# Split operands for the scores and value products of the second block's attention, with scores two units ahead

## Chip, core and metric

The kernel runs on one core of a Trainium2 chip. The metric is the device time of one execution in microseconds, median of the runs. TensorE (PE) multiplies, VectorE (DVE) and ScalarE (ACT) work element by element, GpSimd (POOL) helps, SyncE (SP) issues the transfers.

## What is computed

A first transformer block runs over 256 tokens, then a second block of two layers over the same 256 tokens (x) and 256 context tokens. Everything is float32. The change touches the second block's attention, whose core is:

```python
def latent_attention(q, k, v, k_ctx, v_ctx):
    keys = jnp.concatenate([k_ctx, k], axis=1)
    vals = jnp.concatenate([v_ctx, v], axis=1)
    ...
    s = jnp.einsum('bqhgd,bkhd->bhgqk', q_blk, keys, ...) * scale
    p = jax.nn.softmax(s, axis=-1).astype(vals.dtype)
    return jnp.einsum('bhgqk,bkhd->bqhgd', p, vals)
```

It has 8 heads of 128 dimensions over 2 key-value heads. Queries and keys are normalised per head, those of x are also rotated by position. Layer 0 also attends from the context tokens to themselves.

## The kernel before

Each engine has its own hand-written program; semaphores (`S("name")`) join them. An engine runs its instructions in order, so one that waits holds up all behind it. Matmuls with weights use split operands: ScalarE rounds a float32 tile to a high part (type fp32r), VectorE subtracts it from the original for the low part, and `product` issues three matmuls, high by high, high by low, low by high. Scores, products with values and transposes use plain float32; the records show two matmuls for each such product and one for each transpose.

**Projection (`WIN`).** A layer runs 12 weight chunks (q = 0 to 11), each in two halves of 24 matmuls on PE. Work of other kinds sits between the halves (`within(q)`). Chunks 7 to 10 give the four pairs of query heads, chunk 11 the values and keys rest (`kv10`). After each query chunk ScalarE copies the pair, squares it (HSQ) and multiplies the gain in (`query_pair`). PE sums the squares over the 128 dimensions (`query_sums`, L2447): the squares are the loaded operand and one column of ones streams. VectorE and POOL rotate keys and pairs (`rotated(r)`, L1647 to L1652: shuffle, sine product, a wait for POOL's cosine product, sum). At q = 11 VectorE does `rotated(3)` and, in layer 0, `rotated(4)`, then the low part of a weight chunk (L1233), the reciprocal roots, `maxima(0)` and `gated_lo` (L1715).

**Units.** A unit is a head for 256 queries. Layer 0 has 16: units 0 to 7 with 512 keys, 8 to 15 (context) with 256; layer 1 has 8, with 512. For each unit: PE computes scores (`scores2`, L2508 or L2510); VectorE takes maxima (L1733, L1736); ScalarE takes exponentials with their sums (L1086); VectorE normalises (`normalise2`, L1742 and L1745, tile PB); PE transposes the probabilities (L2615); ScalarE copies them (L1133, tile PT2, two buffers); PE multiplies by the values (`values`, L2522); VectorE copies the result (`attended`, L1751). PE's turn in the loop is scores of u + 1, values of u - 1, transposes of u. In unit 0 PE also transposes the values (L2590) and ScalarE copies them (L1138). During the last two units and after, PE fills in products of the other branch (`hyena_tiles`). Then come the merge, output and feed-forward projections.

The output projection has four chunks (`out`); after the last, VectorE updates X (L1868) and a norm follows.

## Time and profile before

| what | us |
|---|---|
| median of 3 runs | 1856.95 |
| lowest to highest | 1856.34 to 1860.36 |
| the profiled execution, whole | 1852.7 |
| its span in the profile | 1850.9 |
| PE busy in it | 1808.2 (98%) |
| DVE busy | 1078.3 (58%) |
| ACT busy | 796.0 (43%) |
| layer 0's units (first to last transposes) | 762.4 to 823.0 |
| layer 1's units | 1508.0 to 1542.4 |

A busy share tells how long an engine had work in flight. The profiled execution took 4.25 us less than the median, so a sum made on the profile is moved by that much to stand beside the median. In a timeline, the difference between two starts on PE is what an instruction costs its queue; its own duration is longer, since matmuls overlap.

### The profile page before, as it was taken

How to read it: one execution, taken by the hardware profiler on the slowest of the kernel's cores; microseconds unless marked ns; L12 is line 12 of the kernel's file. 1: busy time of each engine (PE TensorE's matmuls, PEld its weight loads, DVE VectorE, ACT ScalarE, POOL GpSimd, SP SyncE). 2: the span in 40 equal slices, each digit the busy share in tenths (PEclk: the TensorE clock that was granted, in tenths of full speed). 3: DMA queues.
4: the chain of work that ended last, by engine and by line, in shares of the span. 5: the costliest groups of instructions: out<-in, count | busy, mean ns of one | idle time of the engine just before them, and what ended most of it. 6: DMA issues, size and time to landing. Idle time of an engine off the chain costs nothing.

```text
span 1850.9 us, 27019 instructions
## 1 busy us (share of the span) xinstructions
PE 1808.2 (98%) x11122; PEld 1552.6 (84%) x11122; DVE 1078.3 (58%) x1268; ACT 796.0 (43%) x1003; POOL 139.3 (8%) x122
## 2 busy tenths in 40 slices
PE   7999998999999999999999999999999999999998
PEld 6889895888998888777878788888888979988898
DVE  5776475677667565654334447754227775466564
ACT  6444435454446433554323422222226455355543
POOL 3000211300004110101000100000001010000000
PEclk9999999999999999999999999999999999999999
DMA  9875487777543321103224268773324423556651
GB/s 280 232 228 208 134 275 258 230 200 214 184 152 120 102 75 63 46 23 110 91 92 112 78 201 256 225 234 112 111 71 154 137 69 105 185 144 182 194 192 68
DMA packets 310626, 284.46 MB, mean 154 GB/s; under 512 B 9108, under 2 KB 290339, under 8 KB 307453
## 3 DMA queue, kind: packets, MB, share of 16 engines
q1 hardware_dynamic: 308394, 278.05, 48.0%
q0 software_dynamic: 1904, 4.89, 0.8%
q8 instruction: 77, 1.26, 0.3%
q14 instruction: 24, 0.20, 0.0%
q10 hardware_dynamic: 227, 0.06, 0.0%
HBM read 280.71 MB, written 2.12 MB: 153 GB/s over the span
## 4 chain that ended last, share of the span: by engine, by line
PE 88%; DVE 4%; ACT 3%; issue 1%; POOL 1%; DMA 1%; ACTq 0%; DVEq 0%; SPq 0%
PE PS L1933 20%; PE PS L1935 20%; PE PS L1934 20%; PE PS L1978 11%; PE PS L1979 6%; PE PS L2522 1%; PE PS L2508 1%; ACT PB L1086 1%; DVE WLO L1233 1%; ACT WHI L754 1%; DMA RAW<-in_ffn_w_gu_dram 1%; PE PS L2105 1%; POOL X L692 1%; PE PS L2615 1%; PE PS L2120 1%
## 5 line engine op out<-in xcount | busy, mean ns | idle before, releaser
L1233 DVE TENSOR_TENSOR WLO<-RAW,WHI 128x2048 fp32r<-128x2048 f32 x209 | 484.9, 2321 | 313.9 <-ACT WHI L754 313.5
L754 ACT ACTIVATE WHI<-RAW 128x2048 fp32r<-128x2048 f32 x209 | 398.9, 1910 | 261.5 <-PE PS L1935 241.5
L1933 PE MATMUL PS<-AHL,WHI 128*128 128x512 f32 (+1 forms) x1424 | 489.9, 344 | 4.2 <-DVE AHL L1363 2.0
L1935 PE MATMUL PS<-AHL,WLO 128*128 128x512 f32 (+1 forms) x1424 | 481.1, 338 | 0.0
L1934 PE MATMUL PS<-AHL,WHI 128*128 128x512 f32 (+1 forms) x1424 | 481.1, 338 | 0.0
L1978 PE MATMUL PS<-AHL,WHI 128*128 128x512 f32 x1056 | 373.6, 398 | 3.8 <-DVE AHL L1363 2.0
L1933 PEld LDWEIGHTS PS<-AHL,WHI 128*128 128x128 f32 x1424 | 269.9, 190 | 42.0 <-issue 9.2
L1979 PE MATMUL PS<-AHL,WLO 128*128 128x256 f32 x1056 | 296.9, 281 | 0.0
L1934 PEld LDWEIGHTS PS<-AHL,WHI 128*128 128x128 f32 x1424 | 270.1, 190 | 29.4 <-issue 1.2
L1935 PEld LDWEIGHTS PS<-AHL,WLO 128*128 128x128 f32 x1424 | 270.0, 190 | 29.2
L1978 PEld LDWEIGHTS PS<-AHL,WHI 128*128 128x128 f32 x1056 | 199.8, 189 | 53.4 <-issue 7.4
L1933 PE MATMUL PS<-SHI,WHI 128*128 128x256 f32 (+1 forms) x704 | 219.9, 312 | 0.8 <-DVE SLO L1239 0.8
L1934 PE MATMUL PS<-SLO,WHI 128*128 128x256 f32 (+1 forms) x704 | 218.0, 310 | 0.0
L1935 PE MATMUL PS<-SHI,WLO 128*128 128x256 f32 (+1 forms) x704 | 217.9, 310 | 0.0
L1979 PEld LDWEIGHTS PS<-AHL,WLO 128*128 128x128 f32 x1056 | 201.4, 191 | 0.1
L1933 PEld LDWEIGHTS PS<-SHI,WHI 128*128 128x128 f32 x704 | 134.3, 191 | 12.1 <-issue 5.0
L1935 PEld LDWEIGHTS PS<-SHI,WLO 128*128 128x128 f32 x704 | 134.3, 191 | 6.8
L1934 PEld LDWEIGHTS PS<-SLO,WHI 128*128 128x128 f32 x704 | 134.3, 191 | 6.7
L1203 ACT ACTIVATE SIL<-PS 128x512 f32<-128x512 f32 x22 | 13.2, 599 | 181.0 <-PE PS L1935 180.9
L1898 DVE TENSOR_TENSOR HB<-SIL,PS 128x512 f32<-128x512 f32 x22 | 15.1, 687 | 92.9 <-ACT SIL L1203 92.9
L836 ACT ACTIVATE GU<-PS 128x512 f32<-128x512 f32 x44 | 26.2, 595 | 98.8 <-PE PS L1979 96.7
L1286 DVE SCALAR_TENSOR_TENSOR LACC<-LRAW,SC,LACC 128x1024 f32<-128x1024 f32 x56 | 68.3, 1278 | 0.0
(305 smaller groups left out, 1885.8 us busy)
## 6 DMA issues: line engine op xcount, KB each, us to landing
RAW<-in_w_in_dram SPq DMA_DIRECT2D x98, 512.0 KB, 4.5
RAW<-in_ffn_w_gu_dram SPq DMA_DIRECT2D x88, 512.0 KB, 5.4
RAW<-in_w_gate_up_dram SPq DMA_DIRECT2D x88, 512.0 KB, 5.1
MRAW<-in_w_mod_dram SPq DMA_DIRECT2D x24, 1024.0 KB, 8.2
LRAW<-in_w_mod_dram SPq DMA_DIRECT2D x48, 512.0 KB, 4.8
RAW<-in_ffn_w_down_dram SPq DMA_DIRECT2D x44, 512.0 KB, 4.3
RAW<-in_w_down_dram SPq DMA_DIRECT2D x44, 512.0 KB, 4.2
RAW<-in_w_out_dram SPq DMA_DIRECT2D x24, 512.0 KB, 4.5
```

The lines of the kernel that those rows point to most:

```text
L692: pool.tensor_tensor(X[:, k, 0:TX], X[:, k, 0:TX], TU[:, k, :], ALU.add).then_inc(S("xu"), 1)
L754: act.activation(WHI[:, c % RING, :], RAW[:, c % RING, :], ACT.Copy).then_inc(S("hi_done"), 1)
L836: act.activation(GU[:, j % RING, :, :], ringw(j)[:, :, TX:TB], ACT.Copy).then_inc(S("gu_lo"), 1)
L1086: act.activation(PB[:, s, t, 0:n], src, ACT.Exp, scale=RC[:, col:col + 1], bias=NM[:, s, t:t + 1], accum_out=SMX[:, s, t:t + 1]).then_inc( ...
L1233: dve.tensor_tensor(WLO[:, c % RING, :], RAW[:, c % RING, :], WHI[:, c % RING, :].bitcast(F32), ALU.subtract)\
L1286: dve.scalar_tensor_tensor(out=LACC[a][:, :, :], in0=raw, scalar=col, in1=LACC[a][:, :, :], op0=ALU.mult, op1=ALU.add).then_inc(S("mod_acc ...
L1933: pe.matmul(out, whi, xhi, start=first, stop=False, skip_group_check=shared)
L1934: pe.matmul(out, whi, xlo, start=False, stop=False, skip_group_check=shared)
L1935: return pe.matmul(out, wlo, xhi, start=False, stop=last, skip_group_check=shared)
L1978: pe.matmul(out[:, b, :], whi, both[:, :, a, 0:TX], start=a == 0, stop=False, skip_group_check=True)
L1979: last = pe.matmul(out[:, b, 0:TX], wlo, both[:, 0, a, 0:TX], start=False, stop=a == KT - 1, skip_group_check=True)
L2105: last = pe.matmul(PS[32 * b:32 * b + 32, 7, :], SC[:, at:at + 32], MRAW[mod_slot(t)][:, b, :], start=t == 0, stop=t == MAIN - 1)
```

## The change

Scores and products with values use split operands. ScalarE makes high queries (QHI, a block b of two heads each), high keys (KHI), and writes PT2 and the transposed values VT2 as high parts; VectorE makes the low parts QKLO (in the place of the originals), PT2LO and VT2LO. PT2 now has one buffer. `attended` moves from VectorE to ScalarE. Scores run two units ahead. The query sums of the first three pairs now load a 32-column selector and stream the squares, each token tile into a group of 32 output partitions of its own; the roots are taken earlier for these (`early_roots`), turned by one transpose (`roots_turned`), and a second reciprocal is added. In layer 1's last output chunk the two output tiles get separate banks, and the first is updated halfway. Cut to its core:

```diff
...
-        VT2 = at("VT2", [P, 8, P], 128 * K)
+        QKLO = at("QKLO", [P, 12, TB], A, F32R)
+        QHI = at("QHI", [P, 4, 2, TX], A + 24 * K, F32R)
+        KHI = at("KHI", [P, 2, TB], 140 * K, F32R)
+        VT2, VT2LO = at("VT2", [P, 8, P], 128 * K, F32R), at("VT2LO", [P, 8, P], 192 * K, F32R)
...
-        PT2 = at("PT2", [P, 2, 4, TX], A + 40 * K)
+        PT2, PT2LO = at("PT2", [P, 4, TX], A + 40 * K, F32R), at("PT2LO", [P, 4, TX], A + 44 * K, F32R)
...
+                return [PS[:, 0, 0:TX], PS[:, 1, 0:TX]]
+            return [ring2(j, n)[:, t, :] for t in range(2)]
...
+                def early_roots():
+                    act.wait_ge(S("h_ss"), 6 * layer + 4)
+                    act.activation(QROOT[0:32 * tq, :], PS[0:32 * tq, 7, TX:TX + P], ACT.Sqrt, bias=EPSC[0:32 * tq, 1:2])\
+                       .then_inc(S("h_std"), 1)
...
+                def keys_hi():
+                    act.wait_ge(S("h_sum"), 5 * layer + 1)
+                    if layer == 0:
+                        act.wait_ge(S("y_fwd"), 4)
+                    act.activation(KHI[:, :, :], QKV[:, 8:10, :], ACT.Copy).then_inc(S("qk_hi"), 1)
+                def queries_hi(b):
+                    heads, tokens = query_block(b)
+                    if b < 4:
+                        act.wait_ge(S("h_sum"), 5 * layer + 2 + b)
+                    if b == 0:
+                        act.wait_ge(S("y_h"), y_done)
+                    elif b >= 4:
+                        act.wait_ge(S("b_s"), u0 + 2 * b - 6)
+                    act.activation(QHI[:, b % 4, :, :], QKV[:, heads, tokens], ACT.Copy).then_inc(S("qk_hi"), 1)
+                def attended(u):
+                    grp, h = units[u]
+                    act.wait_ge(S("b_pv"), u0 + u + 1)
+                    act.activation(QKV[:, h, TX * grp:TX * grp + TX], PS[:, 6 + u % 2, 0:TX], ACT.Copy).then_inc(S("b_o"), 1)
...
+                        early_roots()
+                        queries_hi(1)
...
                         exps(0)
+                        exps(1)
...
+                    if u % 2 == 0 and u and u // 2 + 2 < len(units) // 2:
+                        queries_hi(u // 2 + 2)
...
+                    if u:
+                        act.wait_ge(S("b_pv"), u0 + u)
...
-                        exps(1)
-
+                        queries_hi(2)
+                    else:
+                        attended(u - 1)
+                attended(len(units) - 1)
...
+                def keys_lo():
+                    dve.wait_ge(S("qk_hi"), split_count(layer, -1))
+                    dve.tensor_tensor(QKLO[:, 8:10, :], QKV[:, 8:10, :], KHI[:, :, :].bitcast(F32), ALU.subtract).then_inc(S("qk_lo"), 1)
...
+                    dve.wait_ge(S("qk_hi"), split_count(layer, b))
+                    dve.tensor_tensor(QKLO[:, heads, tokens], QKV[:, heads, tokens], QHI[:, b % 4, :, :].bitcast(F32), ALU.subtract)\
+                       .then_inc(S("qk_lo"), 1)
...
+                def turned_lo(u):
+                    kts = 4 if units[u][0] == 0 else 2
+                    dve.wait_ge(S("b_pt"), u0 + u + 1)
+                    dve.tensor_tensor(PT2LO[:, 0:kts, :], PS[:, 4:4 + kts // 2, :].rearrange("p a (b n) -> p (a b) n", n=TX),
+                                      PT2[:, 0:kts, :].bitcast(F32), ALU.subtract).then_inc(S("b_pl"), 1)
+                    if u == 0:
+                        dve.wait_ge(S("v_ev"), layer + 1)
+                        dve.tensor_tensor(VT2LO[:, :, :], PS[:, 6:8, :].rearrange("p a (b n) -> p (a b) n", n=P),
+                                          VT2[:, :, :].bitcast(F32), ALU.subtract).then_inc(S("b_pl"), 1)
...
                     normalise2(u)
-                    if u + 1 < len(units):
-                        maxima(u + 1)
-                    if u == 0 and layer == 1:
-                        rotated(4)
-                    if u:
-                        attended(u - 1)
+                    if layer == 1 and u < 2:
+                        summed(u + 3)
+                    if u + 2 < len(units):
+                        maxima(u + 2)
+                    if layer == 1 and u == 0:
+                        turned_round(4)
+                    if u % 2 == 0 and u // 2 + 2 < len(units) // 2:
+                        queries_lo(u // 2 + 2)
+                    turned_lo(u)
...
-                        if j == 3 and t == 0 and layer == 0:
-                            dve.wait_ge(S("out_half"), 1)
+                        if j == 3 and t == 0:
+                            dve.wait_ge(S("out_half"), layer + 1)
...
-                            last = pe.matmul(PS[:, 7, TX + h * tq + t:TX + h * tq + t + 1], HSQ[:, h % 2, t * P:t * P + P], ONES[:, 0:1],
-                                             start=True, stop=True)
+                            squares = HSQ[:, h % 2, t * P:t * P + P]
+                            if pair < 3:
+                                last = pe.matmul(PS[32 * t:32 * t + 32, 7, TX:TX + P], SEL[:, 7 - h:39 - h], squares,
+                                                 start=h == 0, stop=h == 5)
...
+                    pe.wait_ge(S("h_std"), 3 * layer + 2)
+                    pe.transpose(PS[:, 7, TX + P:TX + P + 32 * tq], QROOT[0:32 * tq, :], IDENT[0:32 * tq, 0:32 * tq])\
+                      .then_inc(S("h_ss"), 1)
...
+                    pe.wait_ge(S("qk_lo"), split_count(layer, u // 2))
                     for t in range(2):
-                        q = QKV[:, h, TX * grp + t * P:TX * grp + t * P + P]
-                        if grp == 0:
-                            last = pe.matmul(PS[:, 2 * (u % 2) + t, :], q, QKV[:, 8 + h // 4, :], start=True, stop=True)
-                        else:
-                            last = pe.matmul(PS[:, 2 * (u % 2), TX * t:TX * t + TX], q, QKV[:, 8 + h // 4, TX:TB], start=True, stop=True)
+                        q0 = TX * grp + t * P
+                        out = PS[:, 2 * (u % 2) + t, :] if grp == 0 else PS[:, 2 * (u % 2), TX * t:TX * t + TX]
+                        keys = slice(TX * grp, TB)
+                        last = product(out, QHI[:, u // 2 % 4, h % 2, t * P:t * P + P], QKLO[:, h, q0:q0 + P],
+                                       KHI[:, h // 4, keys], QKLO[:, 8 + h // 4, keys], True, True)
...
-                        pe.wait_ge(S("v_ev"), layer + 1)
+                        pe.wait_ge(S("b_pl"), u0 + layer + 2)
                     if u >= 2:
                         pe.wait_ge(S("b_o"), u0 + u - 1)
                     kts = range(4) if grp == 0 else range(2, 4)
+                    out = PS[:, 6 + u % 2, 0:TX]
                     for a, kt in enumerate(kts):
-                        last = pe.matmul(PS[:, 6 + u % 2, 0:TX], VT2[:, 2 * kt + h // 4, :], PT2[:, u % 2, a, :],
-                                         start=a == 0, stop=a == len(kts) - 1)
+                        pe.matmul(out, VT2[:, 2 * kt + h // 4, :], PT2[:, a, :], start=a == 0, stop=False)
+                    for a, kt in enumerate(kts):
+                        pe.matmul(out, VT2LO[:, 2 * kt + h // 4, :], PT2[:, a, :], start=False, stop=False)
+                    pe.wait_ge(S("b_pl"), u0 + layer + u + 2)
+                    for a, kt in enumerate(kts):
+                        last = pe.matmul(out, VT2[:, 2 * kt + h // 4, :], PT2LO[:, a, :], start=False, stop=a == len(kts) - 1)
...
+                    if q == 11:
+                        roots_turned()
                     if 8 <= q <= 11:
                         query_sums(q - 8)
                     if q == 11:
                         scores2(0)
+                        scores2(1)
...
-                scores2(1)
                 for u, (grp, h) in enumerate(units):
                     last_two = u - len(units) + 2
-                    if u and u + 1 < len(units):
-                        scores2(u + 1)
+                    if u + 2 < len(units):
+                        scores2(u + 2)
                     if u:
                         values(u - 1)
                     if u == 0:
                         pe.wait_ge(S("qkv_ev"), 6 * layer + 6)
                     pe.wait_ge(S("b_p"), 2 * (u0 + u) + 2)
+                    if u:
+                        pe.wait_ge(S("b_pl"), u0 + layer + u + 1)
...
```

VectorE at q = 11 of layer 0, before. QKV are queries and keys, BR the rotation's scratch tile, WLO a weight chunk's low part, RC reciprocal roots, NM maxima, HLO the other branch's low part:

```order
L1647 STREAM_SHUFFLE BR<-QKV 128x512
L1649 TENSOR_TENSOR BR<-BR,ROPE 128x512
L1652 TENSOR_TENSOR QKV<-QKV,BR 128x2x256
L1233 TENSOR_TENSOR WLO<-RAW,WHI 128x2048
L1723 RECIPROCAL RC<-STD 128x32
L1733 TENSOR_REDUCE NM<-PS 128x2
L1736 TENSOR_TENSOR NM<-NM,RC 128x2
L1715 TENSOR_TENSOR HLO<-HY,HHI 128x512 x4
L1742 RECIPROCAL RS<-SMX 128x2
```

These begin with the second of two rotations. And in the changed kernel, from the same rotation:

```order
L1708 STREAM_SHUFFLE BR<-QKV 128x512
L1710 TENSOR_TENSOR BR<-BR,ROPE 128x512
L1717 TENSOR_TENSOR QKV<-QKV,BR 128x2x256
L1810 TENSOR_TENSOR QKLO<-QKV,QHI 128x2x256
L1295 TENSOR_TENSOR WLO<-RAW,WHI 128x2048
L1793 RECIPROCAL RC<-PS 128x24
L1796 RECIPROCAL RC<-STD 128x8
L1818 TENSOR_REDUCE NM<-PS 128x2
L1821 TENSOR_TENSOR NM<-NM,RC 128x2
L1818 TENSOR_REDUCE NM<-PS 128x2
L1821 TENSOR_TENSOR NM<-NM,RC 128x2
L1785 TENSOR_TENSOR HLO<-HY,HHI 128x512 x4
```

A low part of queries, a reciprocal and a second maxima came in; another `QKLO<-QKV,QHI` stands ahead of the first of the two rotations.

VectorE in unit 0 of layer 0, changed (before: RS, PB, NM, NM only):

```order
L1827 RECIPROCAL RS<-SMX 128x2
L1830 TENSOR_SCALAR PB<-PB,RS 128x512 x2
L1818 TENSOR_REDUCE NM<-PS 128x2
L1821 TENSOR_TENSOR NM<-NM,RC 128x2
L1810 TENSOR_TENSOR QKLO<-QKV,QHI 128x2x256
L1837 TENSOR_TENSOR PT2LO<-PS,PT_123 128x1024
L1841 TENSOR_TENSOR VT2LO<-PS,VT_119 128x1024
```

Three subtractions now stand behind the maxima and ahead of the next unit's RS.

PE in one of layer 0's later units, changed (before: two scores, four products, eight transposes, in the same turn). KHI and QHI are high parts, QKLO low ones:

```order
L2033 MATMUL PS<-KHI,QHI 128x512
L2034 MATMUL PS<-QKLO,QHI 128x512
L2035 MATMUL PS<-KHI,QKLO 128x512
...
L2631 MATMUL PS<-PT_123,VT_119 128x256 x4
L2633 MATMUL PS<-PT_123,VT2LO 128x256 x4
L2636 MATMUL PS<-PT2LO,VT_119 128x256 x4
L2732 MATMUL PS<-IDENT,PB 128x128 x8
```

The last four products read PT2LO, which VectorE makes after ScalarE's copy; the next transposes stand behind them.

## Rows read from the trace of the kernel before

**Rows 1.** The page, part 4: the chain that ended last, by engine.

```profile
...
PE 88%; DVE 4%; ACT 3%; issue 1%; POOL 1%; DMA 1%; ACTq 0%; DVEq 0%; SPq 0%
...
```

**Rows 2.** Timeline of PE, layer 0's units: start us, us, group xcount, [idle before <-releaser].

```profile
...
762.40 1.04 PE L2615 MATMUL PS<-IDENT,PB 128*128 128x128 f32 x8
...
768.16 1.09 PE L2615 MATMUL PS<-IDENT,PB 128*128 128x128 f32 x8 [0.41 <-DVE PB L1745]
...
773.89 1.04 PE L2615 MATMUL PS<-IDENT,PB 128*128 128x128 f32 x8
...
779.09 1.88 PE L2508 MATMUL PS<-QKV 128*128 128x512 f32 x4
780.80 1.93 PE L2522 MATMUL PS<-PT,VT 128*128 128x256 f32 x8
782.57 1.04 PE L2615 MATMUL PS<-IDENT,PB 128*128 128x128 f32 x8
...
795.56 1.04 PE L2615 MATMUL PS<-IDENT,PB 128*128 128x128 f32 x8
...
```

**Rows 3.** Timeline of PE, layer 0's units of 256 keys.

```profile
...
801.79 0.60 PE L2615 MATMUL PS<-IDENT,PB 128*128 128x128 f32 x4
...
816.18 0.60 PE L2615 MATMUL PS<-IDENT,PB 128*128 128x128 f32 x4
...
```

**Rows 4.** Timeline of PE, layer 1: transposes of the first two units.

```profile
...
1508.02 1.06 PE L2615 MATMUL PS<-IDENT,PB 128*128 128x128 f32 x8 [1.32 <-DVE PB L1745]
...
1513.81 1.09 PE L2615 MATMUL PS<-IDENT,PB 128*128 128x128 f32 x8 [0.41 <-DVE PB L1745]
...
```

**Rows 5.** The chain in order of time, 700 to 860 us: query sums, start us, us.

```profile
...
739.12 1.68 PE PS L2447 x16
...
```

**Rows 6.** The chain in order of time, 1450 to 1660 us: key sums and query sums.

```profile
...
1462.49 0.57 PE PS L2427 x16
...
1481.01 0.79 PE PS L2447 x8
...
```

**Rows 7.** Timeline of PE, rounded operands, 512 columns.

```profile
...
757.05 0.40 PE L1935 MATMUL PS<-AHL,WLO 128*128 128x512 f32 x1
757.28 0.39 PE L1933 MATMUL PS<-AHL,WHI 128*128 128x512 f32 x1
...
```

**Rows 8.** Timeline of PE, rounded operands, 256 columns.

```profile
...
1461.98 0.28 PE L1933 MATMUL PS<-AHL,WHI 128*128 128x256 f32 x1
1462.10 0.28 PE L1934 MATMUL PS<-AHL,WHI 128*128 128x256 f32 x1
...
```

**Rows 9.** Groups by line, 700 to 860 us, DVE and ACT: busy us, mean ns | idle.

```profile
...
L1836 DVE TENSOR_TENSOR MG<-MG,SG 128x1024 f32<-128x1024 f32 x1 | 1.2, 1225 | 5.9 <-ACT SG L1164 5.9
...
L1133 ACT ACTIVATE PT<-PS 128x1024 f32<-128x1024 f32 x8 | 8.1, 1018 | 2.4 <-PE PS L2615 2.4
...
L1133 ACT ACTIVATE PT<-PS 128x512 f32<-128x512 f32 x8 | 4.7, 593 | 4.3 <-PE PS L2615 4.3
...
L1067 ACT ACTIVATE HHI<-HY 128x512 fp32r<-128x512 f32 x4 | 2.2, 616 | 0.0
...
```

**Rows 10.** Timeline of DVE, layer 0, last projection chunk and first units.

```profile
...
749.71 0.01 DVE L1647 LOAD_MASK_SELECT BR<-QKV  x1 [2.40 <-ACT QKV L1034]
...
752.42 0.69 DVE L1652 TENSOR_TENSOR QKV<-QKV,BR 128x512 f32<-128x512 f32 x1 [1.25 <-POOL QKV L729]
...
759.36 0.15 DVE L1742 RECIPROCAL RS<-SMX 128x2 f32<-128x2 f32 x1
...
780.00 0.88 DVE L1745 TENSOR_SCALAR PB<-PB,RS 128x512 f32<-128x512 f32 x2
781.00 1.22 DVE L1733 TENSOR_REDUCE NM<-PS 128x2 f32<-128x1024 f32 x1
...
```

**Rows 11.** Timeline of DVE, layer 1, last output chunk.

```profile
...
1646.71 0.88 DVE L1868 SCALAR_TENSOR_TENSOR X<-PS,MOD,X 128x256 f32<-128x256 f32 x2 [2.23 <-PE PS L1935]
...
```

**Rows 12.** Window in layer 1: busy us of PE, PEld, DVE, ACT, POOL; granted clock.

```profile
...
1650.00:1655.00 5.00, 3.16 (x14) 2.66 (x14) 4.36 (x12) 2.83 (x6) 0.00 (x0) 0.57 0.03 8
...
```

More of the change, by code:

```diff
@@ L397, in ring2, with split_count, query_block, out_tiles @@
             return PS[:, s:s + 2, :] if n == TB else PS[:, s, :].rearrange("p (t n) -> p t n", t=2)
+        def split_count(layer, b):
+            return 9 * layer + 2 + b
+        def query_block(b):
+            return slice(2 * (b % 4), 2 * (b % 4) + 2), slice(TX * (b // 4), TX * (b // 4) + TX)
+        def out_tiles(j, n):
+            if n == TX and j == 3:
+                return [PS[:, 0, 0:TX], PS[:, 1, 0:TX]]
+            return [ring2(j, n)[:, t, :] for t in range(2)]
         def win_out(layer, c):
@@ L1029, in query_pair @@
                         act.wait_ge(S("h_kn"), 2)
-                    act.wait_ge(S("h_ss"), 5 * layer + pair + 1)
+                    act.wait_ge(S("h_ss"), 6 * layer + pair + 1)
                     act.wait_ge(S("qkv_ev"), 6 * layer + pair + 2)
@@ L1091, in _ @@
                     c = FIRST[f"win{layer}"] + q
+                    if q == 11:
+                        queries_hi(0)
                     split_w(None, c + AHEAD)
+                    if q == 9 and layer == 0 or q == 10 and layer == 1:
+                        keys_hi()
                     if layer == 0 and q == 0:
@@ L1653, in rotated @@
                        .then_inc(S("h_sum"), 1)
+                def rotated(r):
+                    turned_round(r)
+                    summed(r)
                 def tapped(q, m0):
@@ L1746, in normalise2 @@
                            .then_inc(S("b_p"), 1)
-                def attended(u):
-                    grp, h = units[u]
-                    dve.wait_ge(S("b_pv"), u0 + u + 1)
-                    dve.tensor_copy(QKV[:, h, TX * grp:TX * grp + TX], PS[:, 6 + u % 2, 0:TX]).then_inc(S("b_o"), 1)
+                def turned_lo(u):
[7 more added lines that the diff above has]
+                                          VT2[:, :, :].bitcast(F32), ALU.subtract).then_inc(S("b_pl"), 1)
                 for q, (kind, m0) in enumerate(WIN[layer]):
@@ L1793, in _ @@
                             rotated(2)
+                            keys_lo()
                     if q == 11:
-                        rotated(3)
+                        queries_lo(0)
                         if layer == 0:
+                            rotated(3)
                             rotated(4)
+                        else:
+                            turned_round(3)
+                        queries_lo(1)
                         split_w(None, FIRST[f"win{layer}"] + q + AHEAD)
@@ L1800, in _ @@
                         maxima(0)
+                        maxima(1)
                         gated_lo()
@@ L2093, in later_rows @@
                         for b in range(4):
-                            last = pe.matmul(PS[32 * b:32 * b + 32, 6, TX * half:TX * half + TX], SEL[:, 5 - x:37 - x], LACC[a][:, b, :],
+                            last = pe.matmul(PS[32 * b:32 * b + 32, 6, TX * half:TX * half + TX], SEL[:, 7 - x:39 - x], LACC[a][:, b, :],
                                              start=part == 0 and x == 0, stop=r == 2, skip_group_check=True)
@@ L2663, in _ @@
                         pe.wait_ge(S("xo"), 2 * KT * layer + 2 * (nt // TX))
-                    out = ring2(j, nt)
                     def first_tile(last):
-                        if layer == 0:
-                            last.then_inc(S("out_half"), 1)
+                        last.then_inc(S("out_half"), 1)
                         norm_sums(9 + 2 * layer, nt // P, SQ2, range(4))
-                    by_columns(None, FIRST[f"out{layer}"] + j, [out[:, 0, :], out[:, 1, :]], AHI2, ALO2, nt,
+                    by_columns(None, FIRST[f"out{layer}"] + j, out_tiles(j, nt), AHI2, ALO2, nt,
                                ready=wait_k("mg_lo", KT * layer) if j == 0 else None, between=first_tile if j == 3 else None)
```

56 lines of the change are left out of this document (32 added, 24 removed).

## Prediction

> **What bounds the kernel now.** I read the page's chain first: 88% of the end-setting chain is PE [rows 1]. So an edit counts by what it does to PE's queue, and elsewhere only where PE comes to wait. Then I read PE's timeline through the units of layer 0. In the steady state scores (start 779.09), products (780.80) and transposes (782.57) stand back to back: 1.71 + 1.77 + 0.87 us, a unit every 4.33 us, with no wait [rows 2]. The first units are slower: transposes start at 762.40, 768.16 and 773.89, steps of 5.76 and 5.73 us, since exponentials, copy and products follow one another there [rows 2]. From the third (773.89) to the eighth (795.56) are five steps, 21.67 us. The 256-key units go from 801.79 to 816.18 in five steps of 2.88 us [rows 3]. Layer 1 starts as layer 0: 1508.02 to 1513.81, 5.79 us [rows 4]. I call the transposes of unit u T(u).
>
> **Part 1, query sums.** A pair in layer 0 now holds PE for 1.68 us (16 records) [rows 5]. The nearest row to the new form is the key sums: also 32 loaded columns, 128 streamed, four output groups, 16 records, 0.57 us [rows 6]. Three pairs save 3 x 1.11 = 3.3 us. VectorE and ScalarE wait on PE in that stretch, so all moves forward. In layer 1 a pair costs 0.79 us [rows 6] and uses two output groups. Bounds per pair: nothing saved, or down to half of 0.57, 0.29. I take half of 0.79 and a little, 0.43: 0.36 each. Only pairs 0 and 1 help, since the wait behind pair 2 is VectorE's; about 0.75 us. The Trainium skill (TensorEngine Tiling (Array Packing), Theoretical Speedup) allows a factor of up to 4 for a dimension of at most 32. By it layer 0's pairs would cost 0.42 us and save 3.8; the row shows a factor of 2.9.
>
> **Part 2, matmuls.** Rounded matmuls start 0.23 us apart with 512 columns [rows 7], 0.12 us with 256 [rows 8]. Scores take 6 x 0.227 = 1.36 us for 1.71, products 12 x 0.12 = 1.44 for 1.77; leaving and entering plain float32 costs about 0.08 us each time: the last matmul starts at 1462.10 [rows 8], the key sums by 1462.49 [rows 6] and not 0.12 later. PE's work in a unit falls to 1.36 + 1.44 + 0.87 + 0.16 = 3.83 us. If PE stayed the bound, each step would gain 0.5 us. It does not, by part 3.
>
> **Part 3, the new loop.** PT2 has one buffer and PT2LO is made from the same PSUM banks that the next transposes write. So this circle closes once per unit: T(u), ScalarE's copy, VectorE's low part, VectorE's normalisation of unit u + 1 (queued behind it), T(u + 1). Transposes take 1.04 us [rows 2] and 0.09 to be seen; the copy 1.02 [rows 9] + 0.04; the low part reads PSUM and SBUF, 1024 elements: the subtraction's nearest row is 1.23 us [rows 9], 1.15 of it in the queue; normalisation 0.20 + 0.88 [rows 10] + 0.06. Sum 4.48 us a step, against 4.33. VectorE's maxima (1.22 us [rows 10], 1.33 with its small product) and a 512-element low part of queries (0.69 us, 0.62 in the queue [rows 10]) fit beside transposes and copy. ScalarE, 43% busy over the span, takes on `attended` and high queries; both lie beside VectorE's part of the circle. With 256 keys the circle is 0.60 + 0.09 [rows 3], 0.59 + 0.04 [rows 9], 0.61, 0.88: 2.81, against 2.88.
>
> **Part 4, the start in layer 0.** `queries_lo(0)` stands ahead of `rotated(3)` on VectorE and needs `queries_hi(0)`, which ScalarE reaches only after the last pair's gain, the release at 749.71 [rows 10]. Before, `rotated(3)` was done by then and only `rotated(4)` was left. So ahead of the first normalisation (759.36 [rows 10]) VectorE's chain gains: high queries 0.62 [rows 9], low queries twice 0.62, a rotation 749.71 to 752.42 + 0.61 = 3.3 [rows 10] and 0.2 of its own wait, a second reciprocal 0.2, a second maxima 1.33. Together 6.9 us: normalisation at 766.3, T(0) at 767.4, for 762.40 now; +5.0. PE stands idle for some of it, while scores of unit 2 go by.
>
> From T(0) to T(1): transposes 1.13, copy 0.92 and value copy 0.92 (queue), `queries_hi(2)` 0.66, and then on VectorE `queries_lo(2)` 0.62, low probabilities 1.15, low values 1.29, for both of which `values(0)` waits, then the products 1.52: 8.2 us for 5.76, +2.45. T(1) to T(2): 4.48 for 5.73, -1.25. To T(7): 5 x 4.48 = 22.4 for 21.67, +0.7. T(7) to T(9): one mixed step 4.2 and 2.81 for 6.23, +0.8. Then five of 2.81: -0.3. Behind it products filled in cover the waits, and the last two products give 0.1. Sum +7.3; with part 1, **+4.0 us in layer 0**.
>
> **Part 5, layer 1.** Only the first half of `rotated(3)` stays ahead, so VectorE's chain grows by low keys 1.15 + 2 x 0.62 + 0.2 + 1.33 = 3.9 and loses the wait for POOL and the sum, 1.25 + 0.61 [rows 10], and 0.2: +1.8. T(0) also needs the copy of kv10, now behind two units' exponentials on ScalarE; both chains end within 0.5 us of each other, and I take +1.7. Less 0.75 from part 1: +0.95. T(0) to T(1) 8.2 for 5.79, +2.4; to T(2) -1.25; four steps +0.6; the last, filled with products, and the end -0.3. **+2.4 us.** Halving the last output chunk's update takes one of two (0.88 us together [rows 11]) off the path: -0.4. The key copy and low keys in layer 0 lie under PE's halves of chunks 9 and 10; uncovered they would cost 2.2 us. The longer way to the first a2_lo adds 0.6 us on ScalarE, under 5.5 us of products.
>
> **Sum.** +4.0 + 2.4 - 0.4 = +6.0 us on the profiled execution's 1852.7. Beside the median, 4.25 us higher, that is **1863 us**, 0.3% slower.
>
> **Rival A, the clock falls.** In the output norm of layer 1, where PE had 3.16 of 5 us of work, the granted clock was 0.57, so that part ran at 1.2 GHz for 2.4 [rows 12]. My schedule leaves PE idle about 1.6, 1.7 and 3.5 us around T(0) and T(1). A clock of 0.57 over 5 us is 4.3 us at half speed; PE's 3.83 us of a unit then take 7.7 for 4.48, and 4.3 us at that rate lose 1.8; with a tail as long again up to 2.9 a layer. Both layers: 1863 + 3.6 to 5.8, about 1868. Against: PE stood idle 1.32 us ahead of layer 1's T(0), and its first step, 5.79 us, is no longer than layer 0's 5.76 [rows 2, 4]. The Trainium skill (TensorE: Matmul & The Clock Gate, The HAM clock gate) says that the array goes to 1.2 GHz when it has been idle; by that rule this is the outcome. Chance 0.2.
>
> **Rival B, the start costs no more than now.** The mechanism: scores two ahead let exponentials and maxima run during the wait, and VectorE, idle there before, takes its subtractions in gaps, so that T(0) to T(1) stays at 5.8 us. That is -2.4 in each layer, 1858: within the noise. The order speaks against it: the subtractions stand in series behind the copies. Chance 0.17.
>
> **Rival C, cheap subtractions (faster).** One mechanism: the low parts cost half of the row's 1.23 us. Then the circle is 3.9 us, T(0) to T(1) loses 1.5, the start 0.5 and 1.1. Layer 0: 6 x 0.55 + 1.5 + 0.5 + 6 x 0.27 = 6.9; layer 1: 5 x 0.55 + 1.5 + 1.1 = 5.3. Sum -12: 1851, faster. It decides from about 0.7 us for 1024 elements on. Against: 512 elements take 0.69 and 1024 take 1.23, proportionally. Chance 0.08.
>
> **Rival D, no gain from the sums** in spite of the key sums: +3.3 + 0.75, 1867. Chance 0.07.
>
> **How the numbers follow.** The forecast keeps 0.48, with its own range of 1860.5 to 1865.5 (some 0.1 us a step over 18 steps, 0.5 for the starts). What a measurement can tell from no change is 0.2%, 3.7 us: 1853.2 to 1860.7. Faster is rival C, 0.08. Same is rival B and a small share of the forecast, 0.24. Slower is the rest, 0.68. The range of 1857.5 to 1869 leaves out C and the far tail of A.
>
> **What would show it.** Right: T(u) steps of 4.4 to 4.6 us in layer 0 with VectorE busy or awaited in each; `QKLO<-QKV,QHI` waiting for ScalarE at the head of chunk 11; T(0) to T(1) near 8.2 us; the first three pairs' sums near 0.6 us. Wrong: steps under 4.2, which would mean that subtraction or copy is cheaper than its row; T(1) less than 7 us behind T(0); an idle gap in chunks 8 to 10 of either layer, which would say that the sums' gain was not handed on; or a granted clock under 0.9 in the units, rival A.

## The result and the profile after

| | us |
|---|---|
| before, median of 10 runs beside the change | 1856.1 |
| after, median of 10 runs | 1865.3 |
| after to before | 1.0048, 95% interval 1.0039 to 1.0057 |
| the profiled execution after, whole (its span) | 1865.7 (1863.9) |

The change costs 9.2 us; forecast were 1863.0 us and a range of 1857.5 to 1869. The two profiled executions lie 13.0 us apart, more than the medians, so I set landmarks. The first is PE's `UNFOLD` product of chunk 8 (706.41 us before, 708.43 after). All the matmuls ahead of it are the same in both, so the 2.0 us there belong to the execution, not to the change. "Net" below means with this shift taken off.

| stretch, us | before | after | forecast of the difference | measured |
|---|---|---|---|---|
| landmark to T(0), layer 0 | 55.99 | 57.69 | +1.7 | +1.70 |
| T(0) to T(1) | 5.76 | 9.45 | +2.45 | +3.69 |
| T(1) to T(2) | 5.73 | 4.46 | -1.25 | -1.27 |
| T(2) to T(7), five steps | 21.67 | 22.29 | +0.7 | +0.62 |
| T(7) to T(9) | 6.23 | 6.99 | +0.8 | +0.76 |
| T(9) to T(14), five steps | 14.39 | 13.97 | -0.3 | -0.42 |
| T(14) to T(15) | 6.78 | 8.31 | -0.1 | +1.53 |
| T(15) to layer 1's T(0) | 685.06 | 687.18 | +0.95 | +2.12 |
| layer 1's T(0) to T(7) | 34.33 | 37.32 | +1.5 | +2.99 |
| from there to the end | 308.55 | 307.81 | -0.4 | -0.74 |

Five of the terms hit within 0.12 us. Of those that were exceeded, three hold stretches of low clock (T(0) to T(1), T(14) to T(15), and layer 1's first steps), and the fourth is the start of layer 1. Without the 2.0 us ahead of the landmark and the 1.5 us at T(14), which did not come back in a second profile (e8), the two profiles lie 9.5 us apart, near the 9.2 of the medians.

The chain of work that ended last, in order of time (start, us, engine and tile), layer 0, after. It shows T(0) at 766.12, then all that stands ahead of the first products, and one steady step (784.49 to 788.95):

```profile
766.12 1.08 PE PS L2732 x8
767.24 0.04 issue
767.28 1.02 ACT PT L1192
768.30 0.92 ACT VT L1197
769.22 0.52 ACT QHI L1118
769.77 0.69 DVE QKLO L1810
770.46 1.14 DVE PT2LO L1837
771.59 1.14 DVE VT2LO L1841
772.73 0.14 issue
772.87 1.20 PE PS L2631 x4
...
784.49 1.11 PE PS L2732 x8
785.62 1.04 ACT PT L1192
786.67 1.22 DVE PT2LO L1837
787.90 0.08 DVE RS L1827
787.98 0.03 issue
788.00 0.89 DVE PB L1830 x2
788.90 0.05 issue
788.95 1.11 PE PS L2732 x8
```

The second half is the circle of the prediction's part 3: transposes, copy, low part, normalisation, 4.46 us (1.13 + 1.05 + 1.23 + 1.05), where [rows 2] have PE's queue without a gap. The first half is part 4: seven pieces in series before a product can start.

Timeline of PE there (start, us, group xcount, idle before and its releaser), and the windows (busy us of PE, PEld, DVE, ACT, POOL, then the granted clock):

```profile
772.87 1.20 PE L2631 MATMUL PS<-PT,VT 128*128 128x256 f32 x4 [3.42 <-DVE VT2LO L1841]
775.57 1.09 PE L2732 MATMUL PS<-IDENT,PB 128*128 128x128 f32 x8
780.03 1.09 PE L2732 MATMUL PS<-IDENT,PB 128*128 128x128 f32 x8 [0.26 <-DVE PB L1830]
...
770.00:775.00 5.00, 2.13 (x10) 2.16 (x11) 4.93 (x8) 1.25 (x4) 0.00 (x0) 0.73 0.01 3
820.00:825.00 5.00, 3.87 (x19) 2.84 (x19) 2.63 (x9) 3.00 (x10) 0.00 (x0) 0.85 0.00 0
1525.00:1530.00 5.00, 4.27 (x22) 4.20 (x23) 3.44 (x7) 0.32 (x1) 0.00 (x0) 0.66 0.01 3
```

After 3.42 us of idle time the twelve first products take 2.70 us (772.87 to 775.57) instead of 1.5, at a granted clock of 0.73 over the window: for part of it the array ran at 1.2 GHz instead of 2.4. The same happened at layer 1's first products, behind 3.59 us of idle time, and in this execution once more behind T(14).

VectorE, after: the head of chunk 11 in layer 0, and layer 1's last output chunk; PE, after: layer 1 between the halves of chunk 11 and its T(0).

```profile
749.14 0.69 DVE L1810 TENSOR_TENSOR QKLO<-QKV,QHI 128x512 fp32r<-128x512 f32 x1 [4.04 <-ACT QHI L1118]
...
1660.17 0.48 DVE L1968 SCALAR_TENSOR_TENSOR X<-PS,MOD,X 128x256 f32<-128x256 f32 x1 [1.83 <-PE PS L2035]
1661.96 0.55 DVE L1410 RECIPROCAL RT<-RT 128x64 f32<-128x64 f32 x1 [1.30 <-ACT RT L816]
...
1507.85 0.47 PE L2033 MATMUL PS<-KHI,QHI 128*128 128x512 f32 x1 [1.40 <-DVE QKLO L1810]
1518.77 1.09 PE L2732 MATMUL PS<-IDENT,PB 128*128 128x128 f32 x8 [0.78 <-ACT QKV L1168]
```

The first low queries wait 4.04 us for ScalarE; that they would wait was forecast. The last update of X (`[rows 11]`, two tiles in one row) is one tile long now.

### The profile page after: what moved, and what is told of

Read it like the earlier page. It is cut to its first block, busy times and chain, and to the rows that moved or that the text cites. A ratio compares the mean times of both kernels' runs of the same rounds, so it can differ in the third digit from the quotient of the medians.

```text
span 1863.9 us, 27384 instructions
## 1 busy us (share of the span) xinstructions
PE 1809.9 (97%) x11252; PEld 1559.2 (84%) x11252; DVE 1103.5 (59%) x1286; ACT 810.8 (44%) x1043; POOL 139.3 (7%) x122
## 3 DMA queue, kind: packets, MB, share of 16 engines
HBM read 280.71 MB, written 2.12 MB: 152 GB/s over the span
## 4 chain that ended last, share of the span: by engine, by line
PE 87%; DVE 6%; ACT 3%; POOL 2%; issue 1%; DMA 1%; ACTq 0%; DVEq 0%; SPq 0%
PE PS L2033 20%; PE PS L2035 20%; PE PS L2034 20%; PE PS L2078 13%; PE PS L2079 6%; PE PS L2732 1%; DVE PT2LO L1837 1%; PE PS L2205 1%; ACT PT L1192 1%; DVE PB L1830 1%; POOL SQ L688 1%; POOL X L710 1%; PE PS L2220 1%; PE PS L2599 1%; PE PS L2582 1%
```

## Experiments

All ratios are to the kernel before on the same chip. Times in us are these ratios on the scale of 1856.1 for the kernel before. "Changed" is the kernel after the change.

| run | ratio | 95% interval |
|---|---|---|
| e1 sums alone | 0.9980 | 0.9971 to 0.9989 |
| e2 normalisation first | 1.0044 | 1.0031 to 1.0056 |
| e3 start order | 1.0055 | 1.0043 to 1.0068 |
| e4 pair 2 behind | 1.0028 | 1.0019 to 1.0036 |
| e5 filled | 1.0037 | 1.0023 to 1.0051 |
| e6 all moves | 0.9969 | 0.9957 to 0.9981 |
| e7 scores split only | 0.9958 | 0.9945 to 0.9972 |
| e8 changed again | 1.0051 | 1.0038 to 1.0065 |
| e9 third product behind | 0.9957 | 0.9943 to 0.9971 |
| e10 scores split, best order | 0.9941 | 0.9926 to 0.9955 |
| e11 two ahead, nothing split | 0.9939 | 0.9926 to 0.9952 |

**e1: the query sums alone**, on the kernel before.

```diff
+                            if pair < 3:
+                                last = pe.matmul(PS[32 * t:32 * t + 32, 7, TX:TX + P], SEL[:, 7 - h:39 - h], squares,
+                                                 start=h == 0, stop=h == 5)
...
+                        early_roots()
...
+                        roots_turned()
```

> The kernel before with the query sums of the change alone: 32-column selector, squares streamed, early roots, the roots turned by one transpose, the second reciprocal. All else is as before. My theory: a pair in layer 0 holds PE for 0.6 us instead of 1.68 (3 x 1.1 = 3.3 us saved), layer 1 saves about 0.7, the second reciprocal and the transposition give 0.3 back. 1856.1 - 3.7 = 1852.4 us. Rival (the gain is not handed on, since another wait ends last ahead of the first transposes): the rows of the sums are as short, but PE waits longer behind them, and the time stays at 1856 us.

0.9980 is 3.7 us, as expected. In the profile T(0) net is 2.9 us earlier and layer 1's T(0) another 0.23. Between chunk 8's and chunk 9's `UNFOLD` product lie 15.22 us for 16.26: a pair saves 1.04 us, nearly the 1.11 of the prediction. The Trainium skill (TensorEngine Tiling (Array Packing), Theoretical Speedup) gives a factor of up to 4; an estimate by it is 1.26 us a pair, and no run here reached it. In layer 1 the gain was 0.23 us and not 0.75: between the `UNFOLD` products on both sides of the first pair's sums lie 5.42 us for 5.55, so a pair saves 0.13 us there and not 0.36.

**e4: the third block's low queries behind unit 0's low parts.** What follows changes the changed kernel.

```diff
+                    if u % 2 == 0 and u and u // 2 + 2 < len(units) // 2:
                         queries_lo(u // 2 + 2)
                     turned_lo(u)
+                    if u == 0:
+                        queries_lo(2)
```

> The changed kernel with the low part of the third query block moved behind the low parts of probabilities and values in unit 0 on VectorE, in both layers. In the changed kernel it waits 2.47 us for ScalarE's high queries, and the two low parts for which the first products wait stand behind it. My theory: the first products start 2.1 us earlier, and since PE is idle 1.3 us instead of 3.4 ahead of them, they run at the full clock, 1.5 us for 2.7. Two layers give 4.2 us by the wait alone and 6.4 with the clock: 1865.3 - 5.5 = 1860 us. Rival for the clock (the low clock there comes from something other than the idle time): the products start 2.1 us earlier but still take 2.7 us, 1861 us. Rival for the order (the value copy ends last): the first products start as late as before, 1865 us.

Timeline of PE in e4, first products:

```profile
770.54 0.71 PE L2633 MATMUL PS<-PT,VT 128*128 128x256 f32 x4 [1.39 <-DVE VT2LO L1841]
```

T(1) stands at 772.05, 1.51 us later. T(0) to T(1) is 6.23 us for 9.45: 2.0 us of waiting and 1.2 us by the clock. In layer 1 the wait is 2.17 us, the clock fell again (0.71 from 1520 to 1525 us), and the step gave 1.0. The time fell by 3.7 us (1.0028 for 1.0048) and not by 5.5: layer 1's wait is only 1.4 us shorter and did not bring back the full clock.

**e5: the idle time filled.**

```diff
-                    for t in range(2):
+                    for t in [0, 1] * (3 if u == 3 else 1):
```

> The changed kernel in which PE computes the scores of unit 3 three times over into the same bank (the same values) while it would stand idle ahead of the first products, in both layers. Nothing waits for these scores before that time is over, so the first products start when they did, but PE's idle time ahead of them falls from 3.4 us to about 0.7. My theory (the idle time takes the clock down): the first products run at the full clock, 1.5 us for 2.7 in layer 0 and about 0.8 us less in layer 1; the granted clock in 5 us around them is 1.0 for 0.73 and 0.66. 1865.3 - 2 = 1863 us. Rival (the low clock at this place comes from something else): first products of 2.7 us again, 1865 us.

PE in e5, first products, and the windows around them:

```profile
772.25 0.71 PE L2631 MATMUL PS<-PT,VT 128*128 128x256 f32 x4 [0.71 <-DVE VT2LO L1841]
773.76 1.04 PE L2732 MATMUL PS<-IDENT,PB 128*128 128x128 f32 x8
...
770.00:775.00 5.00, 4.29 (x29) 3.68 (x28) 4.35 (x7) 0.79 (x3) 0.00 (x0) 1.00 0.00 0
```

With useless work in the gap the clock stays at 1.00, in layer 1 too, and the products take 1.51 us. They start 6.76 us behind T(0), for 6.75 in the changed kernel, so of the way to them only PE's own work in the gap has changed. T(0) to T(2) is 12.67 us; the prediction's 8.2 + 4.48 without a clock term is 12.68. So the idle time is the cause. The Trainium skill (TensorE: Matmul & The Clock Gate, The HAM clock gate) says that an idle array goes to 1.2 GHz; the trace agrees, with 0.73 for the gap left open and 1.00 for the gap filled. The time itself, 1.0037 for the 1.0048 and 1.0051 of the changed kernel, shows it less clearly, since the intervals overlap.

**e8: the changed kernel again.**

> The changed kernel once more, as a control beside the others and to see which stretches of low clock come back. If those in the units belong to the kernel's idle time, they stand again at the first products of layer 0 and of layer 1 (T(0) to T(1) near 9.4 and 9 us); if they were chance, they are gone and the step is 8.2 us. Those outside the units (in the first 300 us) should differ from run to run in place and number. Time: 1.0048 of the kernel before.

Its window at the first products of layer 0:

```profile
770.00:775.00 5.00, 4.02 (x19) 4.05 (x20) 3.08 (x6) 0.00 (x0) 0.00 (x0) 0.50 0.02 3
```

T(0) to T(2) is 14.73 us, in layer 1 14.03 (13.91 and 14.24 in the first profile). The low clock at the first products came back in both layers. The one at 820 us did not: T(14) to T(15) is 6.69 us here, for 8.31.

**e3: low queries behind the rotations.**

```diff
-                        queries_lo(0)
                         if layer == 0:
                             rotated(3)
                             rotated(4)
                         else:
                             turned_round(3)
+                        queries_lo(0)
                         queries_lo(1)
```

> The changed kernel with the first low part of queries moved behind the rotations of pairs 2 and 3 on VectorE (layer 0) and behind the first half of the rotation of pair 2 (layer 1). My theory (VectorE's chain ahead of the first normalisation sets the start; in it stood 4.04 us of waiting for ScalarE's high queries at the head of chunk 11): one rotation, 3.3 us, comes out of the chain in layer 0; PE has 1.4 + 1.5 us of idle ahead of the first transposes there, so 2.5 to 3 us arrive. In layer 1 the copy of the last chunk's result ends last ahead of the first transposes, so nothing to -0.4. 1865.3 - 2.8 = 1862.5 us. Rival (the scores of two units and ScalarE's exponentials set the start): the first transposes come less than 1 us earlier, 1864.5 us or more.

No gain (1866 us for the 1862.5 expected), by two causes. T(0) net is 1.77 us earlier, not 2.5 to 3, since the clock fell to 1.2 GHz at 750 us here; in e9 and e10, with the same order and no fall at that place, T(0) net is 3.40 us earlier than in the changed kernel. And in layer 1 the move was wrong: PE now waited 3.84 us instead of 1.40 for the first low queries between the halves of chunk 11, and the way from T(15) to layer 1's T(0) grew by 2.5 us.

**e2: normalisation ahead of the low part.**

```diff
+                    if u + 1 < len(units):
+                        normalise2(u + 1)
                     turned_lo(u)
```

> The changed kernel with one move on VectorE: in each unit the normalisation of unit u + 1 stands ahead of the low part of unit u's probabilities. That takes the normalisation out of the circle transposes, copy, low part, normalisation, transposes. My theory (the circle sets the step): the circle falls to 1.13 + 1.06 + 1.15 = 3.34 us, below PE's 3.83 and VectorE's own work of about 3.95 (normalisation 1.08, maxima 1.33, low part 1.23, half a low part of queries 0.31), so that the steps of 4.46 us become 3.95 to 4.05, and those of 2.80 us about 2.4. 6 x 0.45 + 6 x 0.4 in layer 0 and 5 x 0.45 in layer 1 are 7.4 us: 1865.3 - 7.4 = 1858 us. Rival (ScalarE's copies or the wait on one buffer PT2 set the step): steps stay within 0.1 us of 4.46 and 2.80, 1865 us.

The steps fell as expected, to 3.99 us, and 2.36 with 256 keys. But in unit 0 the normalisation now stood ahead of both low parts, the first products waited 4.42 us and 4.83 in layer 1, and T(0) to T(1) went to 10.45 and 10.83 us. In the profiles the shorter steps bring some 6 us, and 2.9 of them went there. The time, 1.0044 for 1.0048, shows no gain beyond its interval, and 1864 us is 6 over what I expected.

**e6: the three moves together**, e3's in layer 0 only and unit 0 kept free:

```diff
+                    if u and u + 1 < len(units):
+                        normalise2(u + 1)
                     turned_lo(u)
+                    if u == 0:
+                        normalise2(1)
+                        if layer == 1:
+                            turned_round(4)
+                        queries_lo(2)
```

> The changed kernel with VectorE's order moved in three places: in layer 0 the first low part of queries behind both rotations; in unit 0 the normalisation of unit 1 and the third block's low queries behind the low parts of probabilities and values; from unit 1 on the normalisation of unit u + 1 ahead of the low part of unit u. By the single moves: layer 0's first transposes 5 us earlier; T(0) to T(1) about 6.1 us for 9.45; steps of 4.0 us for 4.46 and 2.4 for 2.80. Layer 0: -5.2 and -10.3; layer 1: T(0) to T(1) 7 us for 9, five steps of 4.0, -5.1. 1865.3 - 20.6 = 1844.7 us, 0.6% under the kernel before. Rival (the gains cover one another, since an earlier start meets another wait, or the clock falls elsewhere): half of it, 1855 us.

0.9969 is 1850.3 us: 15 of the 20.6 us. Layer 0's T(0) to T(15) is 56.03 us for 65.47. Missing are above all 3.4 us at the start of layer 0, where T(0) net is 1.77 us earlier and not 5.2 (the clock fell at 750 us as in e3), and 3 us in layer 1's second step, 7.11 us.

**e9: the last four products behind the next transposes.**

```diff
                     last.then_inc(S("b_tr"), 1)
+                    if u:
+                        values_low(u - 1)
```

> The kernel of all three moves, in which the last four products of a unit (value high parts by low probabilities) now stand on PE behind the next unit's transposes instead of ahead of them; VectorE's next low part waits for them. Two things in layer 1 besides: the low keys stand in the first rotation's wait for GpSimd, and the third block's low queries ahead of the last rotation's first half. In the kernel of all moves a step was 3.99 to 4.05 us. Theory A: that step was a shorter circle, transposes 1.07, copy 1.06, low part 1.28, last four products 0.58, next transposes; then the move takes 0.58 us out of it and the step falls to VectorE's own work, about 3.85 us, or 3.75. Theory B (my earlier one): VectorE's own work sets 3.99; then the steps stay at 3.99 to 4.05. Layer 1's second step falls from 7.11 to about 4.1 us, since the waits of 1.53 and 1.38 us in it go, and its start comes 1.1 us earlier. On the scale on which the kernel before takes 1856.1 and that of all moves 1850.3: A gives 1850.3 - 1.6 - 3 - 1.1 = 1844.6 us, B 1846.2.

The chain in e6, a step with 512 keys, where those products (L2641) stand ahead of the transposes (L2737):

```profile
788.62 0.88 DVE PB L1830 x2
789.50 1.23 DVE PT2LO L1837
790.74 0.04 issue
790.78 0.74 PE PS L2641 x4
791.52 0.55 PE PS L2737 x5
```

In e9 seven steps from T(1) take 26.6 us for e6's 28.1, 3.80 each, and lie between 3.53 and 4.05, the longer ones those with a block's low queries on VectorE, which stands idle nowhere between 779 and 787 us. So part of e6's step was the tail of products, theory A, and the rest VectorE. Layer 1 stayed bad: its T(0) was no earlier (687.45 us from T(15), for 687.50), and its second and third steps took 7.36 and 5.31 us. Its chain names the cause, which I had not seen in the order: the last rotation waits for GpSimd's product (L747 begins only once the shuffle is done), and maxima, normalisation and the low part queue behind its sum:

```profile
1509.34 1.84 POOLq L248
...
1511.28 0.69 DVE QKV L1717
1511.97 1.15 DVE NM L1818
...
1514.30 1.15 DVE PT2LO L1839
...
1515.58 1.49 PE PS L2746 x7
```

**e7: scores split, products plain.**

```diff
-                    for a, kt in enumerate(kts):
-                        pe.matmul(out, VT2LO[:, 2 * kt + h // 4, :], PT2[:, a, :], start=False, stop=False)
...
-                    turned_lo(u)
```

> One half of the change alone: scores use split operands, two units ahead, and the new query sums stand, but products with values use plain float32 as before, with two buffers for PT2 and no low parts of probabilities or values; layer 0's first low queries stand behind the rotations. There is no circle through a low part then, and VectorE has 1.2 us less in a unit. My theory: PE is the bound of a step again, scores 1.36 + products 1.77 + transposes 0.87 + 0.16 of switching = 4.16 us, 2.75 with 256 keys; T(0) to T(1) 5.0 us since nothing stands between the copies and the first products. Layer 0: -5 at the start and -8.2 in the units against the changed kernel, layer 1 -6: 1865.3 - 19 = 1846 us, faster than the kernel before by the sums (3.7), by 0.17 us a step and by the exponentials being early (2 us or more a layer). Rival (the switch between the two kinds of matmul costs more than the 0.35 us saved in scores): steps of 4.3 us and more, 1850 us.

0.9958 is 1848.3 us, 2 over what I expected. The fall of the clock at 750 us is in this profile too and took 1.6 us from the start of layer 0, and T(0) to T(1) is 5.36 and 5.78 us for the 5.0 expected. A step on PE in e7:

```profile
780.00 0.48 PE L2019 MATMUL PS<-KHI,QHI 128*128 128x512 f32 x1
...
781.46 1.90 PE L2617 MATMUL PS<-PT,VT 128*128 128x256 f32 x8
783.19 1.04 PE L2711 MATMUL PS<-IDENT,PB 128*128 128x128 f32 x8
```

Scores 1.46, products 1.73 and transposes 0.79 make 3.98 us, not 4.16: the prediction's sizes without a term for switching, 1.36 + 1.77 + 0.87, are 4.00. PE is the bound again, at the same 3.99 that e6 reached with split products.

**e11: nothing split, only the order.**

```diff
-                        last = product(out, QHI[:, u // 2 % 4, h % 2, t * P:t * P + P], QKLO[:, h, q0:q0 + P],
-                                       KHI[:, h // 4, keys], QKLO[:, 8 + h // 4, keys], True, True)
+                        last = pe.matmul(out, QKV[:, h, q0:q0 + P], QKV[:, 8 + h // 4, keys], start=True, stop=True)
```

> The order of the change without any split operand: new query sums, scores two units ahead, ScalarE copies the attended block, but scores and products are plain float32 as in the kernel before. It tells what running ahead gives by itself, and by its distance from the kernel with split scores what these give. Theory: steps of 4.33 to 4.35 us and 2.88 as before (PE bound), T(0) to T(1) 5.1 to 5.3 us for 5.77 and T(1) to T(2) 4.35 for 5.73, but one more unit of scores (1.71 us) ahead of the first transposes, which in layer 0 fills no idle time. Against the kernel with the sums alone that is about 0 in layer 0 and -1.4 in layer 1: on the scale of 1856.1 for the kernel before 1851 us. Rival (running ahead is the main gain): 1849 us or less. Rival (no gain at all): 1852.4 us, as with the sums alone.

0.9939 is 1844.8 us, 6 under what I expected and past the rival's 1849: the new order is the main gain. PE with 256 keys, first the kernel before, then e11:

```profile
802.23 1.03 PE L2510 MATMUL PS<-QKV 128*128 128x256 f32 x4
803.71 1.13 PE L2522 MATMUL PS<-PT,VT 128*128 128x256 f32 x4 [0.45 <-ACT PT L1133]
804.67 0.60 PE L2615 MATMUL PS<-IDENT,PB 128*128 128x128 f32 x4
```

```profile
798.30 1.09 PE L2606 MATMUL PS<-QKV 128*128 128x256 f32 x4
799.23 1.05 PE L2619 MATMUL PS<-PT,VT 128*128 128x256 f32 x4
800.12 0.60 PE L2713 MATMUL PS<-IDENT,PB 128*128 128x128 f32 x4
```

In the kernel before, ScalarE's copy stands behind exponentials that wait for scores just made, and PE idles 0.45 us a unit. Two units ahead that is gone: 2.26 us for 2.88. With T(0) to T(2) of 9.5 us for 11.5, layer 0's units take 54.7 us for 60.6 and layer 1's 32.0 for 34.3. I had taken 2.88 us for PE's own work.

**e10: e7 with two more moves.**

```diff
+                    if u + 1 < len(units):
+                        normalise2(u + 1)
                     if u % 2 == 0 and u // 2 + 2 < len(units) // 2:
                         queries_lo(u // 2 + 2)
...
+                            turned_round(1)
                             keys_lo()
+                            summed(1)
+                            rotated(2)
```

> The kernel with split scores and plain products, with two more moves on VectorE: the normalisation of unit u + 1 ahead of a block's low queries, and in layer 1 the low keys in the first rotation's wait for GpSimd. Theory: steps stay at 3.98, since PE has no gap in them; T(0) to T(1) loses 0.18 us in layer 0 and 0.59 in layer 1, where the transposes waited for the normalisation; the wait of 1.39 us for the first low queries ahead of layer 1's scores falls to about 0.25, and with it the stretch of low clock behind it may go (another 0.5 to 1 us). On the scale of 1856.1 for the kernel before, 1848.3 - 0.8 - 1.1 - 0.7 = 1845.7 us. Rival (the wait ahead of the scores only moves to the waits behind it): 1847.5 us or more.

T(0) to T(1) is 5.02 and 5.01 us, for 5.36 and 5.78. The wait for low queries in layer 1 fell to 0.25 us, but the turned roots now wait 1.13 us for ScalarE, so the way to layer 1's T(0) stayed (687.39 us): there the rival was right. The low clock behind these waits, which might have gone, stayed as well. PE in e10, the first and the tenth of the twelve matmuls of these scores, and the window:

```profile
1491.86 0.76 PE L2022 MATMUL PS<-KHI,QHI 128*128 128x512 f32 x1 [0.25 <-DVE QKLO L1808]
...
1495.58 0.40 PE L2022 MATMUL PS<-KHI,QHI 128*128 128x512 f32 x1
```

```profile
1490.00:1495.00 5.00, 4.40 (x17) 3.63 (x18) 4.55 (x7) 3.58 (x9) 2.10 (x2) 0.69 0.02 3
```

Nine such matmuls take 3.72 us here and 2.15 at the full clock in layer 0. The result, 0.9941, is that of e11. In the profiles split scores save 0.33 us in each 512-key step and cost 2.1 us on the way to layer 1's T(0), where e11 has 685.27; 1.6 of the 2.1 are this low clock. Neither kernel is shown to be the better one; both beat the kernel before, by 0.6%.

## Why the prediction was right, step by step

- **The total.** The change was forecast at +6.0 us and cost +9.2. That 1863 stands only 2.3 us under the measured 1865.3 is in part luck: it was added to a median of three runs, 1856.95, which lies 0.8 us above that of ten.
- **Query sums, -3.3 and -0.75.** Right in layer 0, 1.04 us a pair for 1.11. The term of layer 1 was mis-sized: 0.13 us a pair for 0.36, 0.23 in all (e1).
- **PE's work of 3.83 us a unit.** The sizes held in sum, but for the switching: I had added 0.16 us for it, and e7's step of 3.98 us has no room for it beside 4.00. Scores alone took 1.46 us for 1.36, and products and transposes less than their rows. It did not enter the sum, since the circle was longer.
- **The circle, 4.48 us.** Measured 4.46, and 2.80 for 2.81. That the hit is so close is in part luck: the low part with its waits took 1.23 us for 1.15, the normalisation 1.05 for 1.14. e2 shows that the circle set the step: with the normalisation taken out, 3.99.
- **Start of layer 0, +5.0 before the sums' gain.** Measured +1.70 net of it, as forecast. That one rotation, 3.3 us, is the larger part is shown by e9 and e10 (3.40 us earlier).
- **T(0) to T(1), 8.2 us.** The chain up to the first products was right, 6.75 us for 6.69; the clock was missing: 9.45 in all. The price of the fall, by e5's 12.67 us for T(0) to T(2), is 1.24 us in the first profile and 2.06 in the second; in layer 1, against e5's 13.06, 1.0 to 1.2. So **rival A's mechanism** was present in both layers, at 2.4 and 3.0 us together for the 3.6 to 5.8 that I gave it. I had set it beside the forecast as a case of its own with 0.2; it belonged in the sum, since its condition, PE idle for 3.5 us, was part of my own schedule. What I held against it, a gap of 1.32 us without a fall, said little about one of 3.5: in e4's layer 0 the products behind a gap of 1.39 us kept the full clock, those behind 3.42 did not.
- **Layer 1's start, +0.95.** Mis-sized: +2.12. 0.5 of it is the sums' missing gain. The rest lies where I had taken both chains to end together. The chain of the kernel after runs through 3.15 us of exponentials of two units and then the copy of the last chunk ([rows 4] have the normalisation there), and PE's wait of 1.40 us between the halves of chunk 11, which I had not counted, moves that copy's input back. e11 separates them in part: it too has the exponentials of two units ahead of that copy, but no low parts, and needs 685.27 us for e1's 684.83. So the sums give 0.2 us on this way, the new order costs 0.4, and 1.9 come in with the split operands; which of their waits gives how much was not separated.
- **Output chunk, -0.4.** From the start of the last update to the reciprocal: 1.79 us for 2.18, right. The update before is in [rows 11], the reciprocal here:

```profile
1648.89 0.55 DVE L1349 RECIPROCAL RT<-RT 128x64 f32<-128x64 f32 x1 [1.30 <-ACT RT L798]
```

- **Rival B** is refuted by T(1) (9.45 us), **rival C** by low parts of 1.14 us in the queue, **rival D** by e1.

With the clock's 2.4 to 3.0 us and 1.2 in layer 1's start, the forecast's +6.0 becomes 9.6 to 10.2, for 9.2 measured. The 1.5 us at 820 us are no fixed part of it: that fall came again in e3, and not in e2, e4, e5 and e8, whose units end in the same way.

What the prediction did not ask is what the change's other half was worth. The new order brings 7.6 us (e11 against e1, give or take 3), the sums 3.7. That order is scores two units ahead together with `attended` on ScalarE and the halved output update; these were not timed apart. Split scores end at nothing that the times can show (e10 against e11, give or take 4 us). Split products, with the low parts in series behind the copies, are most of what turns a gain of 0.4% (e7, which also has another order at the start of layer 0) into a loss of 0.5%; in the best order found for them (e9) they reach e7's time and do not beat it.

## What to carry to other kernels

A cheaper matmul pays only as far as the engines that prepare its operands stay off the loop: write the loop as a circle of transfers between engines, with every single buffer in it, and compare that with PE's work before counting PE's gain. Separate the reordering from the arithmetic and time each alone, since here the order and the query sums held all of the gain. And where the schedule that one has worked out leaves PE idle for microseconds, put the low clock behind it into the sum.

## What the runs showed of the hardware

- The clock can fall where PE is shown busy. In e3, e6 and e7 it fell at 750 us, behind 0.45 us of idle time and the sixteen matmuls of the last pair's sums, which stream one column each; windows of e7 and of e10, which has the same instructions there:

```profile
750.00:755.00 5.00, 5.00 (x20) 4.04 (x20) 4.56 (x7) 2.98 (x6) 0.00 (x0) 0.66 0.15 43
```

```profile
750.00:755.00 5.00, 4.55 (x29) 3.82 (x28) 4.06 (x5) 4.79 (x9) 0.84 (x1) 1.00 0.00 0
```

  It cost 1.6 us: T(0) net lies 0.07 us under the kernel before in e3, 1.70 in e10. What decides between the two was not found. The same goes for layer 1's first scores, which stand behind waits of 0.24 and 1.40 us in the changed kernel: the clock stayed full there in both profiles of the changed kernel and fell in the eight of the others that split scores (0.66 from 1505 to 1510 us in e5).
- In code that is the same in all kernels, low clock came at other places in each execution (30, 220 and 285 us in the first profile after, 300 in the second and in that of the kernel before). Over thirteen profiles the landmark of chunk 8 lies between 704.8 and 708.4 us. A difference of two single profiles is no better than that, which is why the table of the result is by stretches.
- Three rounded matmuls of 512 columns take 0.68 us and a plain float32 product 0.86 [rows 2, 7]. A unit's scores are two such products, so splitting them saves PE 0.35 us and costs VectorE 0.31, half of a block's low queries; splitting its products with values saves 0.33 and costs VectorE 1.15.
